# A four-layer and a two-layer transformer on one core: the first modulation multiplied on TensorE from eight preloaded weight tiles, small loads on three queues

## The reference

```python
cond = jax.nn.silu(c)                                     # (1, 1024)
for i in range(4):
    shift, scale, gate = jnp.split(cond @ ada_w[i] + ada_b[i], 3, axis=-1)   # ada_w[i]: 1024 x 3072
    h = rmsnorm(x, norm_g[i]) * (1 + scale[:, None, :]) + shift[:, None, :]
    y = (mla_mixer, swa_mixer, nsa_mixer)[i % 3](h, ...)  # i = 0: multi-head latent attention
    x = x + gate[:, None, :] * y
x = rmsnorm(x, final_norm_g)
...                                                       # second block: two layers, mixer and feed-forward each
```

## Time and profile before

| | |
|---|---|
| median of 3 runs | 3274.11 us (3269.27 to 3284.66) |
| the profiled execution's own time | 3271.46 us |
| its span in the trace | 3269.8 us |
| PE busy | 2995.6 us, 92% of the span |
| DVE, ACT, POOL busy | 1033.2, 647.4, 876.3 us |
| mean granted clock of PE | 0.952 of full speed |
| first product of the first mixer starts at | 113.63 us |

### The profile page before, as it was taken

How to read it: one execution, slowest core, us unless ns; L and a number is a source line. 1 busy time by engine, 2 the same in 40 slices (tenths; PEclk the granted TensorE clock), 3 DMA queues, 4 the chain that set the end, 5 groups by cost and what they waited for, 6 DMA issues and landing times.

```text
span 3269.8 us, 27834 instructions
## 1 busy us (share of the span) xinstructions
PE 2995.6 (92%) x10138; PEld 1641.9 (50%) x10138; DVE 1033.2 (32%) x2086; ACT 647.4 (20%) x1460; POOL 876.3 (27%) x556
## 2 busy tenths in 40 slices
PE   1799988999999998998788978999999999999997
PEld 1356545566666654554555546444444444444443
DVE  5433345323455634325544155200000232100001
ACT  1123122222233422323223122100000100100000
POOL 4480282057170006605700000282000580000000
PEclk7799999989999999998899898999999999999999
DMA  5441342144131014313300100352222442222222
GB/s 173 141 136 47 97 135 65 55 128 137 46 116 26 27 52 141 110 65 93 91 17 7 57 13 21 101 170 94 76 75 80 135 161 77 64 77 77 77 72 70
DMA packets 267402, 278.05 MB, mean 85 GB/s; under 512 B 39093, under 2 KB 240167, under 8 KB 267175
## 3 DMA queue, kind: packets, MB, share of 16 engines
q1 hardware_dynamic: 239655, 176.04, 17.9%
q0 software_dynamic: 27648, 100.68, 9.9%
HBM read 274.59 MB, written 2.10 MB: 85 GB/s over the span
## 4 chain that ended last, share of the span: by engine, by line
PE 86%; DVE 8%; ACT 2%; DMA 2%; issue 1%; SPq 0%; DVEq 0%; PEld 0%; ACTq 0%; PEldq 0%
PE psum L673 44%; PE psum L815 10%; PE psum L1265 9%; PE psum L700 3%; PE psum L1100 2%; PE psum L789 2%; PE psum L1131 2%; PE psum L1086 2%; PE psum L717 2%; PE psum L801 2%; DVE ada_sum L1854 1%; PE psum L937 1%; PE psum L938 1%; PE psum L1136 1%; DVE probs L1980 1%
## 5 line engine op out<-in xcount | busy, mean ns | idle before, releaser
L673 PE MATMUL psum<-h,ring 128*128 128x512 f32 (+1 forms) x3216 | 1390.2, 593 | 32.8 <-ACT h L1394 30.3
L673 PEld LDWEIGHTS psum<-h,ring 128*128 128x128 f32 x3216 | 616.3, 193 | 768.3 <-issue 753.5
L600 POOL DMA_DIRECT2D ada_ring<-in_ada_w x192 | 113.1, 589 | 1799.7 <-DVE gains L1868 1560.1
L616 POOL TENSOR_TENSOR ada_sum<-ada_sum,ada_ring 128x1024 f32<-128x1024 f32 x168 | 397.3, 2365 | 13.2
L815 PE MATMUL psum<-og,ring 128*128 128x512 f32 x768 | 334.8, 595 | 2.2 <-DVE og L2396 1.9
L612 POOL TENSOR_TENSOR ada_ring<-ada_ring,cond 128x1024 f32<-128x1024 f32 x168 | 320.0, 1905 | 5.5 <-POOL ada_sum L616 1.4
L1265 PE MATMUL psum<-arena,ring 128*128 128x512 f32 x704 | 302.5, 592 | 0.0
L815 PEld LDWEIGHTS psum<-og,ring 128*128 128x128 f32 x768 | 145.3, 191 | 182.8 <-issue 179.2
L1265 PEld LDWEIGHTS psum<-arena,ring 128*128 128x128 f32 x704 | 133.8, 190 | 168.4 <-issue 168.4
L2406 DVE TENSOR_TENSOR arena<-psum,arena 128x512 f32 x44 | 30.4, 692 | 573.3 <-PE psum L673 573.3
L2027 DVE SCALAR_TENSOR_TENSOR x<-psum,mods,x 128x512 f32<-128x512 f32 x64 | 48.1, 751 | 483.0 <-PE psum L1265 272.2
(11 more groups left out here) (265 smaller groups left out, 2764.8 us busy)
## 6 DMA issues: line engine op xcount, KB each, us to landing
ada_ring<-in_ada_w POOLq DMA_DIRECT2D x192, 512.0 KB, 4.1
ring<-in_ffn_w_gate SPq DMA_DIRECT2D x22, 1024.0 KB, 5.3
ring<-in_ffn_w_up SPq DMA_DIRECT2D x22, 1024.0 KB, 5.3
ring<-in_ffn_w_down SPq DMA_DIRECT2D x32, 704.0 KB, 4.6
ring<-in_sc_w_in SPq DMA_DIRECT2D x12, 1024.0 KB, 5.2
ring<-in_mla_w_in SPq DMA_DIRECT2D x10, 1024.0 KB, 5.4
ring<-in_ada_w SPq DMA_DIRECT2D x8, 1024.0 KB, 5.5
ring<-in_mla_w_out SPq DMA_DIRECT2D x8, 1024.0 KB, 5.2
```

What stands on the lines that cost most here:

```text
L600: pool.dma_start(ada_ring[:, i % 2, :], w[k * P:(k + 1) * P, first(part)]).then_inc(arrived[i % 2], n.give(f"ada_in{i % 2}", 16))
L616: step = nc.gpsimd.tensor_tensor(total, total, piece, ALU.add)
L673: m = pe.matmul(tile.at[:, part], lhs(k), rhs(k), start=(k == 0), stop=(k == K - 1))
```

## The change

The first 2048 modulation columns are no longer multiplied on DVE. All eight weight tiles of 256 columns are loaded at once, each with a semaphore of its own, into buffers that are empty at that time: two in `og`, three in `h`, three in the arena. PE multiplies them with the condition vector directly (`first_columns`): 16 outputs of 128, each a sum of 8 products with a 128x128 weight tile stationary and one column of `cond` moving, all into one PSUM tile. DVE adds the bias (now 16 columns) and forms the gains after the reciprocal of the norm. The gate columns, still made by POOL, are summed by PE inside the first mixer, after its first four products (`first_gate_columns`).

SP now issues a small piece of the constants (the identity and the ones), `x`, two weight tiles, the rest of the constants and six weight tiles. ACT issues the three condition rows and the five broadcasts, POOL the other 18 row loads ahead of its first fetch. DVE copies the turned tiles of `x` out instead of ACT, and the angles come after those copies. The zeroing product ahead of the sum of squares is replaced by a start flag.

```diff
 ROW_GROUPS = [
-    [("norm_g", 32), ("final_norm_g", 8), ("mla_q_norm_g", 4), ("mla_kv_norm_g", 2), ("c", 8), ("c_2", 8),
...
+    [("c", 8), ("c_2", 8), ("c_ctx_2", 8)],
...
+        first_slots = [og[:, 0:2048], og[:, 2048:4096]] + [h[:, :, :].rearrange("p k n -> p (k n)")[:, 2048 * i:2048 * i + 2048]
+                                                           for i in range(3)] + [view(5120 + 2048 * i, 2048) for i in range(3)]
...
+            def first_weights(i):
+                sp.dma_start(first_slots[i].rearrange("p (k n) -> p k n", k=KT), rows_of(A["ada_w"][0])[:, :, 256 * i:256 * i + 256]
+                             ).then_inc(S[f"first_in{i}"], 16)
+
+            sp.dma_start(cst[:, 0:FIRST_CONSTS], const[:, 0:FIRST_CONSTS]).then_inc(S["ident_in"], 16)
             sp.dma_start(x_tok, A["x"].rearrange("b (j p) d -> p (b j) d", p=P)).then_inc(S["x_in"], 16)
...
+            for put, src in late_rows:
+                pool.dma_start(put, src).then_inc(S["rows_in"], 16)
             pool.wait_ge(S["cond_ready"], 1)
...
+            def first_columns():
+
+                tile = next_tile()
+                pe.wait_ge(S["cond_ready"], 1)
+                for i in range(FIRST_SLOTS):
+                    pe.wait_ge(S[f"first_in{i}"], 16)
+                    for c in range(2):
+                        for k in range(KT):
+                            m = pe.matmul(tile.at[:, 2 * i + c:2 * i + c + 1], w8(first_slots[i], P * c)(k), cond[:, k:k + 1],
+                                          start=(k == 0), stop=(k == KT - 1))
+                m.then_inc(S["tile_done"], 1)
+
+            def first_gate_columns():
+
                 pe.wait_ge(S["ada_step"], KT)
-                column_sums(next_tile(), range(24), True)
+                column_sums(next_tile(), range(16, 24), True)
...
             sum_squares(KT - 1)
-            first_mods()
-            mla()
+            pe.wait_ge(S["rows_in"], 16 * len(late_rows))
+            for g in range(1, len(ROW_GROUPS)):
+                turn_rows(g)
+            first_columns()
+            pe.wait_ge(S["consts_in"], 16)
+            mla(True)
...
-                dve.wait_ge(S["mods_ready"], n.now("mods_ready"))
+                if job == 0:
+                    first_columns()
+                else:
+                    dve.wait_ge(S["mods_ready"], n.now("mods_ready"))
```

More of the change, by code:

```diff
@@ L291, in build, with row_loads @@
         arena = sb("arena", [P, 16384])
-        row_loads = sum(2 if name.endswith(("q_norm_2", "k_norm_2")) else 1 for m in ROW_GROUPS for name, _ in m)
+        def row_loads(groups):
+            loads = []
+            for g in groups:
+                r = 0
+                for name, nr in ROW_GROUPS[g]:
+                    src = A[name]
+                    if name in ("hy_q_norm_2", "hy_k_norm_2"):
+                        loads += [(rows[r:r + 1, g, 64 * half:64 * half + 64], src) for half in range(2)]
+                    else:
+                        flat = src
+                        while len(flat.shape) > 1:
+                            flat = flat.flatten()
+                        loads.append((rows[r:r + nr, g, :], flat.rearrange("(r c) -> r c", c=P)))
+                    r += nr
+            return loads
+        early_rows, late_rows = row_loads([0]), row_loads(range(1, len(ROW_GROUPS)))
         class Depth:
@@ L709, in sum_squares @@
                 pe.wait_ge(S["sq_ready"], n.take("sq_ready"))
[L710 to L712 removed]
+                pe.matmul(SB[0][:, 0:part], ones, sq[:, i % 2, 0:part], start=first, stop=True,
                           skip_group_check=True).then_inc(S["sq_done"], 1)
@@ L1841, in copy_tile, with first_columns, first_gate_columns @@
                 return tile
[L1843 to L1851, removed]
-                        settle(nc.vector.tensor_scalar(total, w[:, 0, :], cond[:, 0:1], None, ALU.mult))
-                        for k in range(1, KT):
-                            step = nc.vector.scalar_tensor_tensor(total, w[:, k, :], cond[:, k:k + 1], total, ALU.mult,
-                                                                  ALU.add)
-                            if k < KT - 1:
-                                settle(step)
-                        step.then_inc(S["slot_summed"], n.give("slot_summed"))
+            def first_columns():
+                tile = next_tile()
+                done(tile)
+                nc.vector.tensor_tensor(mods[:, 0, 0:16], tile.at[:, 0:16], col("ada_b", 0, 16), ALU.add
+                                        ).then_inc(tile_used[tile.bank], 1)
+                evacuated(tile)
+                settle(nc.vector.scalar_tensor_tensor(gains[:, 0, :], mods[:, 0, 8:16], 1.0, col("norm_g", 0, 8), ALU.add,
+                                                      ALU.mult))
+            def first_gate_columns():
+                tile = next_tile()
+                done(tile)
+                nc.vector.tensor_tensor(mods[:, 0, 16:24], tile.at[:, 16:24], col("ada_b", 16, 8), ALU.add
+                                        ).then_inc(tile_used[tile.bank], 1)
+                evacuated(tile)
+                dve.sem_inc(S["mods_ready"], n.give("mods_ready"))
             def mod_columns(job, g):
@@ L2450, in block2_vector, with copy_rows @@
                 final_norm(col("final_norm_2", 0, 8))
+            def copy_rows(g):
+                r = sum(nr for _, nr in ROW_GROUPS[g])
+                copy_tile(cols[:, g, 0:r], r)
+            copy_rows(0)
+            for k in range(KT):
+                copy_tile(x[:, k * T:(k + 1) * T])
+            for g in range(1, len(ROW_GROUPS)):
+                copy_rows(g)
             dve.wait_ge(S["consts_in"], 16)
```

102 lines of the change are left out of this document (41 added, 61 removed).

## The result

| | before | after |
|---|---|---|
| median of 7 runs each | 3284.29 us (3269.27 to 3291.85) | 3258.00 us (3255.31 to 3258.99) |
| the profiled execution's own time | 3271.46 us | 3258.99 us |
| its span | 3269.8 us | 3257.2 us |
| mixer's first product | 113.63 us | 82.80 us |
| from there to the end | 3156.2 us | 3174.4 us |

The ratio is 0.9932, interval 0.9917 to 0.9946: faster by 0.7%, 22 us (18 to 27 by the interval; the two medians lie 26 us apart). The forecast was 3242 with a range of 3217 to 3255, so the time lies above the range. The two profiled executions differ by 12.5 us only, though the mixer starts 30.8 us earlier.

A forecast was written before the change was run, and what follows sets the result against it. PE bounds the kernel from the mixer on; ahead of it, loads and DVE do. 17.2 + 0.7 - 1.5 + 12.0 + 3.3, less 1.8, gives 29.9 us off 3271.46: 3242, range 3217 to 3255.

The forecast's parts named there:

- The head: All ahead of the mixer's first product: `x` on PE at 10 instead of 27.2, mixer at 81.8 instead of 113.63 us.
- its stage: PE's transposes and sums of squares for `x`: 16 us instead of 16.75, with bounds of 13 and 16.8.
- the new products: PE's 256 records ahead of the mixer: 31 at the high clock, 225 at the low, 52.3 us, ending at 79.8.
- the gap behind them: Between last column and mixer: 2.03 us instead of 5.38, as the reciprocal, 3.35 us, is done earlier under cover.
- The gate columns: Sixteen records inside the first mixer: they add 1.8 us, 3.5 at the low clock, and wait for nothing.
- The rival of a clock that stays up: New products run wholly at the high clock in 29.2 us; 22.5 us less, about 3219 us; chance 0.10.
- The slower rival: POOL's 18 row loads each wait for their landing, so the new products start at 72.5; 3287 us; chance 0.04.
- late weights: Weight tiles for the new products land after 73 us; at 125 GB/s products end 16 us later, 3258; chance 0.08.
- 3271.46 - 29.9 = 3242: Whole kernel: the profiled execution's time less the summed gain of 29.9 us gives the forecast, which had chance 0.72.
- From there to the end the two traces have the same length within 5 us plus 1.8: From the mixer's start onward: nothing changes beyond 5 us, apart from the 1.8 us added by the gate columns.
- The rival "Other": Later layers: shifts of clock and of POOL's traffic, either way by up to 15 us; chance 0.06.
- large cover: POOL's next layer starts 38 us later against PE's program, but its next sums are read only at about 373.

The follow-up runs named there:

- e2: The changed kernel again, unchanged, for a second trace and more runs: median 3256.61 us, ratio 0.9922 to the kernel before.
- e10: The changed kernel once more, unchanged, for a third trace on another chip: median 3255.91 us, ratio 0.9916 to the kernel before.
- e5: The changed kernel with 128 equal moving columns instead of one in the 128 new products: median 3233.54 us, ratio 0.9860 to the kernel before.
- e1: The kernel before, again and unchanged, for a second trace: median 3279.3 us in 12 executions, ratio 1.000.
- e6: As e5, and the column sums of POOL's parts move 128 columns too: 3207.25 us, ratio 0.9771 to the kernel before.
- e3: The changed kernel with 64 equal moving columns instead of one in the 128 new products: median 3229.98 us, ratio 0.9850 to the kernel before.

## Why the prediction was right and wrong

**The head was right, term by term, in the first trace.** `x` starts at 10.81 (said 10), its stage takes 17.0 us (said 16), the rows follow in 1.1 us (said 1.5) without a wait for POOL's loads, the new products start at 28.94 (27.5) and take 51.7 us (52.3), with the 31 records at the high clock exactly as put down, which is luck (e2 and e10 had some 4, an estimate from 13.3 us for 64 records at 0.114 and 0.213), and the gap behind them is 2.17 us (2.03). The mixer starts at 82.80, and at 85.4 and 85.1 in e2 and e10; 81.8 was said, with 77 to 87 around it. The gate columns took 1.68 us on the chain (1.8) and waited for nothing: POOL was done at 68.11.

**The clock was the right question.** The rival of a clock that stays up would have needed 1.00 in the stretch from 32.4 to 80.6; there it was 0.50. That the clock sets the price and not the form of the product is shown by e5 and by the first 31 records. The rule of the Trainium skill that was weighed there ("TensorE: Matmul & The Clock Gate", section "Why this matters for your kernels"), by which an engine kept busy keeps its clock, does not hold for products with one moving column: PE was busy 48.20 of 48.20 us at 0.50.

**The slower rival and late weights are out.** POOL issued its 18 row loads one behind the other, 0.48 to 0.70 us each, done at 10.58, without waiting for a landing; they landed 5.5 to 7.5 us after their issue, the last some 10 us before PE turned them. SP, ahead of PE at all times, had issued the last weight tile by 37.9. The rival of late weights had put the time at 3258, which is what was measured, but PE never waited between tiles: the match is chance.

**The step that failed is the sum's base: "3271.46 - 29.9 = 3242".** The gain was worked out with care, but the number that it was taken from is that of an unusually short execution. From the median of all 57, 3279.9, the same 29.9 give 3250, 8 us higher; the stated range, moved by the same 8 us, would be 3225 to 3263 and would hold the measured 3258. The forecast missed by 16 us: 8 of them are this base, more if one takes the 3284.29 of the seven runs in the table, and the rest is gain that did not come. The text noted 2.65 us between the profiled execution and the median of three runs, and took the scatter of these (15 us between the lowest and the highest) into neither the base nor the range. e1 and the executions beside it showed that 3271 is at the edge, and that the mean granted clock goes with it.

**The other step, which cost the gain, is "From there to the end the two traces have the same length within 5 us plus 1.8".** It was 18.2 in the first pair, 8.4 on average over five traces. By the medians it is 2.8 to 5.5, and five traces do not settle which. Of these 8.4, 1.8 are the gate columns, 5.2 are idle time of PE, and the waits for the query weights of the two latent-attention mixers are 5.1 longer. The rival "Other", at 0.06, named shifts of POOL's traffic in the later layers, but with no place and no sum. The prediction said of POOL's later fetches that they have a large cover, which is true for what is read from them; it did not ask what they run into. The mixer's work on PE now meets the fetches at another point, and PE waits some 2 us longer for four small loads that a 512 KB fetch follows by 0.20 to 0.57 us (3.11 to 4.84 us, against 1.13 to 2.93). Why the fetches fall there more often after the change also in the second of these mixers, a thousand microseconds on, where both kernels' POOL starts anew from the same signal, is not shown. 1.4 us of busy time stay unassigned.

**The sum as measured.** 29.1 us at the head (113.5 on average to 84.4), less 8.4, is 20.7; the ratios, 0.9916 to 0.9932, say 22 to 28 us. The forecast of 29.9 was too high by what came in behind the mixer's start and by the head's own scatter: in e2 and e10 the clock fell about half a microsecond into the new products (13.34 us for the first 64 records where the first trace has 10.73), and the mixer started at 85.4 and 85.1.

## What to carry to other kernels

Work a forecast out against several executions, not against the one that was profiled, and look at how their mean granted clock goes with their time before setting a range. A stage of matrix-vector products on TensorE cost almost twice its price at the low clock (0.213 against 0.113 us a record), and at some places the products behind it paid too (29.39 against 27.70 us for 64, e5 and e6). It need not be so: behind the new products the mixer's first 64 took 29.78 us in the changed kernel and 29.40 in e5, since in e5 too the clock stood at 0.50 from 62 to 64 us, behind a gap of 2.17 us. Where the product costs the same with 128 moving columns as with one, as here, moving the vector 128 times side by side costs nothing, and in the traces of e5 and e6 the clock stayed up through the new products. When a stage moves, look not only at whether each background transfer is still in time, but at which foreground loads it will now be issued beside.

## What was not expected of the hardware

With one moving column and with 64 the clock fell to 0.50 while PE was busy throughout. With 64 that seems to happen in some executions and not in others of the same kernel: the only trace of e3 (3260.77 us, mean clock 0.950) shows it, and for the shortest ones (3228.14 us, 0.960) only their time and mean clock speak. With 128 it happened in neither of the two traces, at 0.113 us a record. The same kernel, unchanged, scatters by 25 us (3270.84 to 3296.39, on three chips) with a mean granted clock of 0.944 to 0.952. In the changed kernel the loads queued on SP moved 382 GB/s from 33 to 45 us together with POOL's fetches; SP's own issue of a 1 MB tile then took 4 to 5 us on average (14.17 us for three, single ones 0.50 to 6.89), where the issue of `x`, 2 MB, took 0.40 in the kernel before.
